# Hybrid residual block with expert retrieval: 56 instead of 48 tokens by gathered rows, key choice begun in the query projection, one compare for both one-hots

## The reference

```python
q = (xb @ w_q).reshape(T, PEER_HEADS, 2, PEER_HALF)          # 8 heads, 2 halves of 128
sc = jnp.einsum('thcd,hckd->thck', q, sub_keys)              # 128 keys per half
s1, i1 = lax.top_k(sc[:, :, 0], 16); s2, i2 = lax.top_k(sc[:, :, 1], 16)
cand = (s1[..., :, None] + s2[..., None, :]).reshape(T, 8, 256)
best, ci = lax.top_k(cand, 16)
idx = e1 * 128 + e2                                          # 128 experts per token
g = jax.nn.softmax(best)
act = gelu(einsum('td,thkd->thk', xb, u_tab[idx]))           # rows of a 16384 x 2048 table
return einsum('thk,thkd->td', g * act, v_tab[idx])           # rows of a second one
```

## Time and profile before

| | us |
|---|---|
| median of 3 runs | 1778.72 (1778.35 to 1779.86) |
| the profiled execution | 1775.03 |
| its span | 1772.9 |
| PE busy in it | 1743.1 (98%) |
| DVE busy | 1424.3 (80%) |
| ACT busy | 931.0 (53%) |
| POOL busy | 410.6 (23%) |

### The profile page before, as it was taken

The page is one execution under the profiler, slowest core; times in us unless marked ns, Lnnn a source line. Parts: engine busy times, 40 slices in busy tenths (PEclk is TensorE's granted clock), DMA queues, the critical chain, the costliest instruction groups (busy, mean ns, idle before and its releaser), DMA issues. The chain is left out here.

```text
span 1772.9 us, 28848 instructions
## 1 busy us (share of the span) xinstructions
PE 1743.1 (98%) x10950; PEld 1653.4 (93%) x10950; DVE 1424.3 (80%) x2151; ACT 931.0 (53%) x1400; POOL 410.6 (23%) x294
## 2 busy tenths in 40 slices
PE   9999999999999999999999999999999999999997
PEld 7887778778999999999999999999999999999997
DVE  5545786475579899999999998588888998888995
ACT  5444564453456554555555555555555555555553
POOL 0002300020142133111111112023433333343331
PEclk9999999999999999999999999999999999999999
DMA  7665445677566677777677778899999999999992
GB/s 245 210 183 161 143 148 170 193 234 237 175 219 218 218 256 243 248 244 228 227 231 231 233 233 314 256 335 367 353 359 356 354 321 356 365 363 405 368 349 91
DMA packets 127026, 462.59 MB, mean 261 GB/s; under 512 B 14736, under 2 KB 14832, under 8 KB 126240
## 3 DMA queue, kind: packets, MB, share of 16 engines
q1 hardware_dynamic: 95760, 347.65, 59.0%
q0 software_dynamic: 30992, 112.67, 17.1%
q10 hardware_dynamic: 144, 0.52, 0.1%
HBM read 455.73 MB, written 5.05 MB: 260 GB/s over the span
## 5 line engine op out<-in xcount | busy, mean ns | idle before, releaser
L1597 PE MATMUL PS<-W,HI 128*128 128x416 f32 x2048 | 436.9, 353 | 2.1 <-ACT HI L674 1.4
L1557 PE MATMUL PS<-xT,HI 128*128 128x416 f32 x2048 | 438.1, 356 | 0.0
L674 ACT ACTIVATE HI<-V_RAW 128x1024 fp32r<-128x1024 f32 x256 | 271.6, 1061 | 284.1 <-PE PS L1597 152.2
L1597 PEld LDWEIGHTS PS<-W,HI 128*128 128x128 f32 x2048 | 365.0, 189 | 7.2 <-ACT HI L674 1.6
L1557 PEld LDWEIGHTS PS<-xT,HI 128*128 128x128 f32 x2048 | 365.8, 189 | 2.3
L1129 DVE TENSOR_TENSOR V_LO<-V_RAW,HI 128x2048 fp32r<-128x2048 f32 x128 | 293.0, 2289 | 59.7 <-ACT HI L674 53.5
L674 ACT ACTIVATE HI<-RING_RAW 128x1024 fp32r<-128x1024 f32 x256 | 269.5, 1053 | 50.8 <-DMA RING_RAW<-u_t 49.7
L1136 DVE TENSOR_TENSOR RING_LO<-RING_RAW,HI 128x1024 fp32r<-128x1024 f32 x232 | 274.6, 1218 | 6.8 <-ACT HI L674 6.7
L811 DVE TENSOR_TENSOR LO<-RAW,HI 128x1024 fp32r<-128x1024 f32 x132 | 163.0, 1237 | 136.4 <-PE PS L1330 99.9
L1563 PEld LDWEIGHTS PS<-xT,RING_LO 128*128 128x128 f32 x2048 | 268.3, 191 | 4.1 <-DVE RING_LO L1136 2.0
L1602 PEld LDWEIGHTS PS<-W,V_LO 128*128 128x128 f32 x2048 | 269.3, 191 | 1.9 <-DVE V_LO L1129 0.9
(11 more groups left out here) (207 smaller groups left out, 1656.4 us busy)
## 6 DMA issues: line engine op xcount, KB each, us to landing
RING_RAW<-u_t SPq DMA_DIRECT2D x256, 512.0 KB
V_RAW<-peer_v SPq DMA_DIRECT2D x256, 512.0 KB
RAW<-w_in SPq DMA_DIRECT2D x80, 512.0 KB, 3.6
RAW<-w_out SPq DMA_DIRECT2D x32, 512.0 KB, 4.3
RAW<-wq_t SPq DMA_DIRECT2D x32, 512.0 KB, 4.8
x_spill<-X POOLq DMA_DIRECT2D x2, 1024.0 KB, 5.3
X1R<-x_spill POOLq DMA_DIRECT2D x8, 256.0 KB
X<-x SPq DMA_DIRECT2D x3, 512.0 KB, 8.4
```

Of the source, the lines that this page charges most:

```text
L674: nc.scalar.activation(HI[:, n % HI_SLOTS, :], raw_of(n), ACT.Copy).then_inc(top_ready, 1)
L1557: return mm(PS[:, j % S_BANKS, 0:2 * ND].rearrange("p (a t) -> p a t", a=2), HI[:, n % HI_SLOTS, kk * P:(kk + 1) * P], xT[:, k, :, 0:ND], ...
L1597: return mm(PS[:, V_BANKS[i], 0:2 * ND].rearrange("p (a t) -> p a t", a=2), HI[:, v % HI_SLOTS, i * P:(i + 1) * P], weights_of(v), start=v ...
```

## The change

1. The last 56 tokens (NS) go by gathered rows, in two rounds of 32 and 24; ND is 200. Round A packs four tokens' shares on 128 partitions (32 groups), round B five on 120 (26 groups); 58 groups make 232 halves. Each round does its dots, its own gelu, then its sums. 72 halves are in scoring, 160 in the value stage.
2. The query projection is written out instead of looped. PE scores the keys of each pair of columns there for the first tile (`pair_scores`), ACT copies them out, and DVE does the first 12 pieces of choice there, one every two units. Two of the four key loads move ahead of other work in POOL's queue. DVE waits once for the saved rows of x before the first of these units.
3. With 12 pieces done, the other 70 take steps 1 to 47. Halves start at step 29; spreading starts at step 51, 50 batches. POOL does 16 low halves instead of 24.
4. DVE makes both one-hots by one compare of 1024 columns; ACT then multiplies the second by the gates, four activations of 128 columns (`gates_into`), in its own stream.

```diff
-NA, NB_ = 32, 16
+NA, NB_ = 32, 24
 NS = NA + NB_
 ND = T - NS
-GROUPS_A, GROUPS_B = P * NA // P, P * NB_ // P
+PICKS = PH * TOPK
+ROWS_A, ROWS_B = P // NA, P // NB_
+PB = ROWS_B * NB_
+GROUPS_A, GROUPS_B = PICKS // ROWS_A, -(-PICKS // ROWS_B)
 NG = GROUPS_A + GROUPS_B
-PICKS = PH * TOPK
...
-CHOICE0 = 2
-GATES_AT = (20, 48)
-PICKS_AT = (31, 58)
-ROWS_SAVED_AT, ROWS_BACK_AT = 32, 35
+EARLY = 12
+CHOICE0 = 1
+
+
+def piece_steps():
+
+    steps, j = [-1] * EARLY, CHOICE0
+    while len(steps) < 2 * PIECES:
+        steps += [j] * min(2 - j % 2, 2 * PIECES - len(steps))
+        j += 1
+    return steps
+
+
+PIECE_STEPS = piece_steps()
+PIECE_COUNT = {j: PIECE_STEPS.count(j) for j in range(NKEYS)}
+PLAIN_STEP = {j: PIECE_COUNT[j] > 0 and all(k % PIECES in PLAIN for k in range(2 * PIECES) if PIECE_STEPS[k] == j)
+              for j in range(NKEYS)}
+BEST_PIECE = HC + 2 + PH
+GATES_AT = tuple(PIECE_STEPS[o * PIECES + BEST_PIECE] + 1 for o in range(TT))
+PICKS_AT = tuple(PIECE_STEPS[o * PIECES + PIECES - 1] + 2 for o in range(TT))
+ROWS_SAVED_AT, ROWS_BACK_AT = PICKS_AT[0] + 1, PICKS_AT[0] + 4
 TOKB = 4
 N_BATCH = ND // TOKB
-SPREAD0 = 60
+SPREAD0 = PICKS_AT[1] + 2
...
-HALF_STEPS = list(range(40, SPREAD0, 3)) + list(range(SPREAD0, SPREAD_END, 2)) + list(range(SPREAD_END, NKEYS - 7))
+ROOM = [j for j in range(ROWS_BACK_AT + 3, SPREAD0) if PIECE_COUNT[j] == 0 or PLAIN_STEP[j]]
+HALF_STEPS = sorted(ROOM + [j for j in range(SPREAD0, SPREAD_END) if j % 4] + list(range(SPREAD_END, NKEYS - 7))
+                    + list(range(SPREAD_END, NKEYS - 7, 4)))
 FREE_UNITS = [u for u in range(9, 250) if u not in (NKEYS - 2, NKEYS - 1)]
 HALF_UNITS = [FREE_UNITS[i * len(FREE_UNITS) // (HALVES - len(HALF_STEPS))] for i in range(HALVES - len(HALF_STEPS))]
-LAST_DOT = HALF_UNITS[2 * NG - 1 - len(HALF_STEPS)]
-FIRST_B_DOT = HALF_UNITS[2 * GROUPS_A - len(HALF_STEPS)]
-FIRST_B_SUM = HALF_UNITS[2 * NG + 2 * GROUPS_A - len(HALF_STEPS)]
+A_DOTS, A_SUMS = 2 * GROUPS_A, 4 * GROUPS_A
+B_DOTS, B_SUMS = A_SUMS + 2 * GROUPS_B, A_SUMS + 4 * GROUPS_B
+A_GELU_AT = HALF_STEPS[A_DOTS - 1]
+B_GELU_AT = HALF_UNITS[B_DOTS - 1 - len(HALF_STEPS)]
...
+def half_of(k):
+
+    if k < A_SUMS:
+        return k < A_DOTS, k % A_DOTS // 2, k % 2
+    return k < B_DOTS, GROUPS_A + (k - A_SUMS) % (2 * GROUPS_B) // 2, k % 2
...
+            def keys(q):
+                pool.dma_start(KEYS[:, 4 * q:4 * q + 4, :], keys_t[:, 4 * q:4 * q + 4, :]).then_inc(keys_ready[q], 16)
+
+            pool.wait_ge(used, WQ0 + 1)
+            keys(0)
...
-            with act.Fori(0, N_WQ // 4 - 1) as i:
-                for r in range(4):
-                    hi_at(i, 4, WQ0 + 4 + r)
+
+            def pair_scores_out(q):
+
+                act.wait_ge(sc_done, q + 1)
+                nc.scalar.activation(SC[:, TILE_ORDER[0], 2 * q:2 * q + 2, :],
+                                     PS[:, 4 + q % 4, q // 4 * 2 * NKEYS:(q // 4 + 1) * 2 * NKEYS]
+                                     .rearrange("p (a b) -> p a b", b=NKEYS), ACT.Copy).then_inc(sc_out, 1)
+
+            for m in range(4, N_WQ):
+                hi(WQ0 + m)
+                if m >= 9 and m % 4 == 1:
+                    pair_scores_out((m - 9) // 4)
...
+            def gates_into(b):
+
+                act.wait_ge(compared, b + 1)
+                for i in range(TOKB):
+                    t = b * TOKB + i
+                    ins = nc.scalar.activation(ONE[:, 1, i, :], ONE[:, 1, i, :], ACT.Copy, scale=EG[:, 2, t:t + 1])
+                ins.then_inc(ones, 1)
...
+                if 0 <= j + 1 - SPREAD0 < N_BATCH:
+                    gates_into(j + 1 - SPREAD0)
+                if j == 0:
+                    pair_scores_out(7)
+                if j == 2:
+                    tile_scores_out()
...
-            with dve.Fori(0, N_WQ // 4 - 1) as i:
-                query_pair(i)
...
+            dve.wait_ge(xs_saved, 16)
+            for m in range(2, N_WQ + 2):
+                if m < N_WQ:
+                    lo(WQ0 + m)
+                c = (m - 3) // 2
+                if m % 2 and c >= 0:
+                    dve.wait_ge(used, WQ0 + 2 * c + 2)
+                    add_halves(QTQ[:, c, :], c % 2)
+                if m % 2 == 0 and 0 <= (m - 8) // 2 < EARLY:
+                    piece()
...
-                v.tensor_tensor(ONE1[:], IOTA[:].unsqueeze(1).broadcast_to([P, TOKB, NKEYS]),
-                                EG[:, 0, b * TOKB:(b + 1) * TOKB].unsqueeze(2).broadcast_to([P, TOKB, NKEYS]), ALU.is_equal)
-                for i in range(TOKB):
-                    t = b * TOKB + i
-                    ins = v.tensor_scalar(ONE2[:, 4 * i:4 * i + 4, :], IOTA[:].rearrange("p (q c) -> p q c", q=4),
-                                          EG[:, 1, t:t + 1], EG[:, 2, t:t + 1], ALU.is_equal, ALU.mult)
-                ins.then_inc(ones, 1)
+                t0 = b * TOKB
+                v.tensor_tensor(ONE[:], IOTA[:].unsqueeze(1).unsqueeze(1).broadcast_to([P, 2, TOKB, NKEYS]),
+                                EG[:, 0:2, t0:t0 + TOKB].unsqueeze(3).broadcast_to([P, 2, TOKB, NKEYS]), ALU.is_equal)\
+                    .then_inc(compared, 1)
...
-                if j in HALF_STEPS:
-                    half_rows(HALF_STEPS.index(j))
+                for k in range(len(HALF_STEPS)):
+                    if HALF_STEPS[k] == j:
+                        half_rows(k)
...
+            def pair_scores(q):
+
+                pe.wait_ge(tile_out, 2 * q + 2)
+                pe.wait_ge(keys_ready[q // 2], 16)
+                if q >= 4:
+                    pe.wait_ge(sc_out, q - 3)
+                for c in (2 * q, 2 * q + 1):
+                    at0 = (q // 4 * 2 + c % 2) * NKEYS
+                    last = mm(PS[:, 4 + q % 4, at0:at0 + NKEYS],
+                              QTQ[:, c, TILE_ORDER[0] * P:(TILE_ORDER[0] + 1) * P], KEYS[:, c, :], start=True, stop=True)
+                last.then_inc(sc_done, 1)
+
+            for m in range(N_WQ):
+                n = WQ0 + m
+                high_ready(n)
+                if m >= 4 and m % 2 == 0:
+                    pe.wait_ge(tile_out, m // 2 - 1)
+                column_unit(n, m // 2 % 2, low_ready(n),
+                            (lambda k: pe.wait_ge(tr_lo, 16 + max(2, k // 2 + 1))) if m < 2 else None)
+                if m >= 5 and m % 4 == 1:
+                    pair_scores((m - 5) // 4)
...
-                    last = mm(PS[:, G_BANK + b % 2, t * NKEYS:(t + 1) * NKEYS].rearrange("p (q c) -> p q c", q=4),
-                              ONE1[:, t, :], ONE2[:, 4 * t:4 * t + 4, :],
+                    last = mm(PS[:, G_BANK + b % 2, t * NKEYS:(t + 1) * NKEYS], ONE[:, 0, t, :], ONE[:, 1, t, :],
...
-                if n in (3, 7):
-                    key_scores(n // 4)
+                if n == 1:
+                    pair_scores(7)
+                if n == 3:
+                    tile_scores()
```

184 lines of the change are left out of this document (77 added, 107 removed).

## The result

| | before | changed |
|---|---|---|
| median of 4 runs each | 1778.53 us (1774.9 to 1779.9) | 1881.70 us (1879.2 to 1887.1) |
| ratio | | 1.058, interval 1.0562 to 1.0597 |
| profiled execution, its span | 1775.03, 1772.9 | 1879.23, 1877.4 |
| PE busy | 1743.1 (98%) | 1767.4 (94%) |
| DVE, ACT, POOL busy | 1424, 931, 411 | 1454, 985, 401 |

What follows compares the result with a forecast made beforehand. PE was taken to bound the kernel. Terms of -28.7 + 1 + 8 + 9 + 3 gave -7.7 us, taken as -7, so from a median of 1778.72 the forecast was 1771.5 us, range 1760 to 1786.

Steps and rivals of the forecast that it cites:

- Narrower products: On PE throughout: high products shrink from 416 to 400 columns, gaining 27 us; low ones gain none; unit 2.357 us.
- rival D: On PE, low products shrink with their columns too, saving 13.7 us, for 1758 us; chance 0.06.
- Query projection: While PE projects queries, twelve choice pieces fit into DVE's time; cost 0, up to 2 us.
- rival E: In the query projection, moved choice pieces hold up PE's units by half of their 20 us: +10, 1781; chance 0.05.
- Choice in scoring: Scoring steps 0 to 50: DVE's lag peaks at about 11 us against cover 3, so PE loses 8 us (6 to 11).
- Spreading: Spreading the gates, 50 steps: a closed loop through ACT takes 5.85 us and costs 9 us (0 to 20).
- B: Gate spreading: the loop through ACT does not bind, as scalings cost near 0.20 us: -9 us, 1763; chance 0.12.
- C: Stretches paced by DVE cost double, through lag feeding the next or delaying ACT: +8 us, 1779.5; chance 0.10.
- Value stage apart from the form of the load: Value stage: usual gathers fit the 8.7 us limit, a dozen beside late loads exceed it; cost 3 us (0 to 25).
- rival A: Value stage: gathers over 8.7 us bind; gain gone at 9.05, 13 to 22 us cost at 9.2 to 9.4; chance 0.17.

Runs made afterwards that it cites:

- e9_all: Changed kernel with round B loads of 128 rows, a fourth buffer, no half in value-stage units 120 to 129, scaled compares back on DVE: 1764.0 us, ratio 0.9926.

## Why the prediction was wrong, point by point

- **The step that failed** is in the part on the value stage, a cost put at nothing: "that 104 of them fill 120 partitions and not 128 leaves their length as it is, since all partitions work at once". That is true of DVE's half (1.23 us) and was said of it alone. I never asked the same of the load that fills those 120 partitions. For DMA I weighed bytes (353 to 364 GB/s), as if the form of a transfer had no price, and no bound from a row stood there. It cost 100.7 us (1881.7 against 1781.0 with 128 rows), by packets of 235 ns in place of 159 ns, PE's waits behind them and a clock at its lower level for 82 us. No rival held it either.
- **The nearest row was there.** The kernel before has loads of 16 rows, and the window from 1136 to 1147 us shows them at a DMA share of 1.03 and 232 GB/s. I had read the value stage as one window, which averages over it.
- **Narrower products: right.** A unit takes 2.35 us (2.357 forecast), 0.056 us less than before, 28.7 us over 512 units. High products take 1.47 us per eight (1.49), low ones 0.88 as before, so rival D falls. Rows of the changed kernel for the earlier trace rows:

```profile
1078.03 1.04 PE L1606 MATMUL PS<-xT,RING_LO 128*128 128x200 f32 x8
1078.91 1.63 PE L1600 MATMUL PS<-xT,HI 128*128 128x400 f32 x8
1080.38 1.04 PE L1606 MATMUL PS<-xT,RING_LO 128*128 128x200 f32 x8
```

- **Query projection: right.** PE does not wait for a piece there, so rival E falls. The stretch began 2.1 us later than before, behind work that the change does not touch, and lasted 94.2 us in place of 89.9: 3.2 us are the key scores that moved here, the rest is a piece of 3.4 us at the lower clock (e9_all has no such piece and takes 93.2 us). At the start of scoring PE waited 1.9 us for the pair copies, where I had 1. What such a wait can cost more is seen in the 32 key scores behind it, first in the changed kernel, then in e9_all:

```profile
472.06 5.46 PE L1590 MATMUL PS<-KEYS,QTQ 128*128 128x128 f32 x32 [1.93 <-ACT SC L688]
469.28 3.84 PE L1614 MATMUL PS<-KEYS,QTQ 128*128 128x128 f32 x32 [1.93 <-ACT SC L710]
```

The wait is the same, 1.93 us, but the first execution's granted clock from 472.0 to 477.3 us is 0.68 and the second one's stays at 1.00.
- **Choice in scoring: right mechanism and place, and the size right by luck.** PE waits for DVE's low halves at 628, 639 and 651 us, steps 33, 35 and 37; I had steps 28 to 37. Steps 28 to 38 take 59.9 us where eleven steps want 51.9, so the cost is 8.0 us, my number. But I had meant 8 us of waits. The waits are 3.8 us (up to 6.3 in the other kernels with 56 tokens); from the last of them on PE is at a clock of 0.50 for 6.8 us, an estimated 3.4 us of cost, for which I had no term. It answers to the earlier trace rows:

```profile
628.30 1.14 PE L1606 MATMUL PS<-xT,RING_LO 128*128 128x200 f32 x8 [0.88 <-DVE RING_LO L1173]
...
650.88 2.03 PE L1606 MATMUL PS<-xT,RING_LO 128*128 128x200 f32 x8 [2.22 <-DVE RING_LO L1173]
```

- **Spreading: right.** Forecast loop 5.85 us and 9 us of cost; measured 5.78 on average and 7.6. Four scalings hold ACT 1.19 us (1.16 forecast). I took the loop as constant; it grows from 5.69 to 5.88 as the gate product in it grows from some 200 to 396 elements (0.36 to 0.56 us). Rivals B and C fall.
- **Value stage apart from the form of the load: rival A, under-rated.** I took 3 us. With 128 rows the value stage took 637.7 us, 23.5 more than the 614.2 of the kernel before with narrower units: 6.2 us of them in the middle (8.1 less 1.9), some 17 in the rest, where 14.0 us are waits for the weights. The load took 9.3 to 9.6 us where DVE waited; A put the turning point at 9.05 and 13 to 22 us of cost at 9.2 to 9.4. I had set a limit of 8.7 against one quiet load of 8.37, which is 4% of room. The middle was missing from the sum: DVE's backlog meets its eight reductions there, and PE needs their places at once.
- **In sum:** without the form of the load the kernel takes 1781.0 us, inside the range and 9.5 us above the forecast, by the value stage: scoring starts 4.7 us later than before and lasts 3.2 us less than the terms for it add up to, together 1.5 us.

## What to carry to other kernels

When a change alters the shape of a transfer, price the transfer and not just the engine that uses it: the share of the DMA engines, times 16 engines and the window's length, divided by the packets in it gives ns per packet, and a DMA share of 1.0 at a lower GB/s than the same kernel reaches elsewhere is the sign that form, not demand, is the limit. Pad an uneven gather to all 128 partitions, even with rows that nobody reads, and move loads over few partitions to a place where the buffers of the main stream are full. Where a loop has 4% of room against one measured latency, give its rival the larger chance, and add a buffer before adding work. Count a wait of PE at more than its own length, since the clock may fall behind it.

## What the runs showed of the hardware that I had not expected

- Indirect loads of 120, 112 or 96 rows of 4096 bytes slow **all** transfers beside them: packets of 4096 bytes from a median of 159 ns to 235, 202 and 207 on the queue of the raw tiles, the rate from 352 to 371 GB/s down to 272 to 308. It begins with the first such load and ends with the last (352, 285, 352, 280 GB/s in one execution).
- Direct loads of 16 rows do the same while they run: 232 GB/s, 0.588 x 16 x 11 us / 411 packets = 252 ns for a packet of the other queue.
- A load of 128 rows comes with 16 packets of 4 bytes, one of 120 rows with 24, by count in a window.
- PE's granted clock fell to its lower level (0.50) for pieces behind PE's waits: 81.9 us of the value stage in the changed kernel, 6.8 with loads of 128 rows, none in the kernel before. Between 1600 and 1840 us, where PE was idle for 41 of 240 us, the mean is 0.90. After the same wait of 1.93 us it fell in one kernel's execution and not in another's, so the runs do not show what decides it.
